# Gate and up units of a two-layer FFN: one 512-column product for the high and low activations, halves summed by VectorE

## The reference

```python
D_MODEL, SEQ, D_FF = 1024, 256, 2816

def swiglu(u, w_gu, w_down):
    gate, up = jnp.split(u @ w_gu, 2, axis=-1)      # w_gu: 1024 x 5632
    return (jax.nn.silu(gate) * up) @ w_down        # w_down: 2816 x 1024

for i in range(DEPTH):                              # DEPTH = 2
    ...                                             # mixer and memory attention
    u = rmsnorm(x, ffn_pre_g[i])
    x = x + rmsnorm(swiglu(u, ffn_w_gu[i], ffn_w_down[i]), ffn_post_g[i])
```

## Time and profile before

| | |
|---|---|
| median of 3 runs | 969.23 us (968.77 to 969.78) |
| the profiled execution | 969.12 us, its span 967.3 us |
| PE busy | 929.6 us, 96% of the span |
| PEld busy | 860.7 us, 89% |
| DVE busy | 562.4 us, 58% |
| ACT busy | 487.9 us, 50% |
| HBM read | 162 MB, 169 GB/s over the span |
| mean granted TensorE clock | 0.986 of full |
| gate and up units of layer 0 | about 353 to 480 us of the span |
| gate and up units of layer 1 | about 770 to 899 us |

### The profile page before, as it was taken

How to read it: one execution, slowest core, us unless ns; L and a number is a source line. 1 busy time by engine, 2 the same in 40 slices (tenths; PEclk the granted TensorE clock), 3 DMA queues, 4 the chain that set the end, 5 groups by cost and what they waited for, 6 DMA issues and landing times.

```text
span 967.3 us, 15639 instructions
## 1 busy us (share of the span) xinstructions
PE 929.6 (96%) x6624; PEld 860.7 (89%) x6624; DVE 562.4 (58%) x645; ACT 487.9 (50%) x670; POOL 36.8 (4%) x51
## 2 busy tenths in 40 slices
PE   8999999989999989999999999999999699999996
PEld 7999987868899889999988899987998599999885
DVE  6788465874565575555544754675754645554443
ACT  6565567854545564344433554666645534434332
POOL 1000001220000000000000220000000000000000
PEclk9999999999999999999999999999999699999999
DMA  8866452234653465555555697434643345555651
GB/s 262 270 191 190 131 162 82 91 126 134 208 186 126 130 210 183 173 175 188 191 184 194 211 272 216 132 130 131 219 143 115 114 141 192 188 174 174 194 197 44
DMA packets 121061, 163.80 MB, mean 169 GB/s; under 512 B 4076, under 2 KB 106916, under 8 KB 121012
## 3 DMA queue, kind: packets, MB, share of 16 engines
q1 hardware_dynamic: 117684, 151.99, 48.4%
q0 software_dynamic: 3328, 11.10, 3.9%
HBM read 162.01 MB, written 1.07 MB: 169 GB/s over the span
## 4 chain that ended last, share of the span: by engine, by line
PE 84%; DVE 9%; ACT 4%; issue 2%; DMA 1%; SPq 0%; POOL 0%; DVEq 0%; ACTq 0%
PE bank L443 76%; DVE w_lo L1142 2%; DVE ntmp L1205 1%; PE bank L740 1%; PE bank L711 1%; DVE x L1208 1%; DVE ntmp L1184 1%; ACT ntmp L851 1%; PE bank L637 1%; PE bank L543 1%; DMA d_pair<-in_ssm_d_dram 1%; DVE stats L1173 1%; DVE stats L1175 1%; PE bank L795 1%; PE bank L785 0%
## 5 line engine op out<-in xcount | busy, mean ns | idle before, releaser
L1142 DVE TENSOR_TENSOR w_lo<-w_raw,w_hi 128x2048 fp32r<-128x2048 f32 x135 | 308.5, 2290 | 225.1 <-ACT w_hi L829 225.0
L443 PE MATMUL bank<-actT_hi,w_hi 128*128 128x256 f32 x1280 | 365.1, 285 | 3.3 <-DVE actT_lo L1192 1.6
L443 PE MATMUL bank<-actT_lo,w_hi 128*128 128x256 f32 x1280 | 363.4, 284 | 0.0
L443 PE MATMUL bank<-actT_hi,w_lo 128*128 128x256 f32 x1280 | 363.4, 284 | 0.0
L829 ACT ACTIVATE w_hi<-w_raw 128x2048 fp32r<-128x2048 f32 x135 | 256.7, 1907 | 105.8 <-DMA w_raw<-in_ffn_w_down_dram 52.6
L443 PEld LDWEIGHTS bank<-actT_hi,w_hi 128*128 128x128 f32 x1280 | 247.0, 193 | 5.3 <-issue 4.6
L443 PEld LDWEIGHTS bank<-actT_lo,w_hi 128*128 128x128 f32 x1280 | 247.0, 193 | 0.1
L443 PEld LDWEIGHTS bank<-actT_hi,w_lo 128*128 128x128 f32 x1280 | 246.9, 193 | 0.0
L443 PE MATMUL bank<-w_lo,hT_hi 128*128 128x512 f32 x176 | 68.5, 389 | 0.0
L443 PE MATMUL bank<-w_hi,hT_hi 128*128 128x512 f32 x176 | 68.5, 389 | 0.0
L443 PE MATMUL bank<-w_hi,hT_lo 128*128 128x512 f32 x176 | 68.5, 389 | 0.0
(11 more groups left out here) (209 smaller groups left out, 1279.6 us busy)
## 6 DMA issues: line engine op xcount, KB each, us to landing
w_raw<-in_ffn_w_gu_dram SPq DMA_DIRECT2D x44, 1024.0 KB, 5.1
w_raw<-in_ffn_w_down_dram SPq DMA_DIRECT2D x22, 1024.0 KB, 4.9
w_raw<-in_ssm_w_in_dram SPq DMA_DIRECT2D x20, 1024.0 KB, 5.3
w_raw<-in_mem_w_kv_dram SPq DMA_DIRECT2D x16, 1024.0 KB, 5.5
w_raw<-in_ssm_w_out_dram SPq DMA_DIRECT2D x8, 1024.0 KB, 4.9
w_raw<-in_mem_w_q_dram SPq DMA_DIRECT2D x8, 1024.0 KB, 5.2
w_raw<-in_mem_w_o_dram SPq DMA_DIRECT2D x8, 1024.0 KB, 4.9
w_raw<-in_w_kv_dram SPq DMA_DIRECT2D x8, 1024.0 KB, 5.9
```

What stands on the lines that cost most here:

```text
L443: ins = pe.matmul(dst, a, b, start=first and n == 0, stop=last and n == len(passes) - 1, skip_group_check=True)
L1142: dve.tensor_tensor(lo[:, s, :], raw[:, s, :], hi[:, s, :].bitcast(F32), ALU.subtract).then_inc(w_lo_done, 1)
```

## The change

The activations now stand as one tensor `actT` with high and low side by side for each k-tile (512 columns). `pair_unit` replaces `t_unit` in the gate and up units: for each column block and k-tile one matmul of 512 columns (high weights against high and low activations) and one of 256 columns (low weights against the high activations) that adds to the second half. Each column block takes a PSUM bank of its own, so a unit fills banks 0 and 1 or 2 and 3 in turn. The product is the sum of the two halves of a bank; VectorE makes that sum with one `tensor_reduce` for each unit, into `gate` or `hval`. Silu then works on `gate` in SBUF, and the product of the two on `hval` in SBUF. Every `t_out` of these units comes from VectorE.

```diff
@@ freed_by
     if name in ("gu0", "gu1"):
-        return "dve" if i % 2 else "act"
+        return "dve"
@@ placement
-        actT_hi = place("actT_hi", [P, KD, S], F32R)
-        actT_lo = place("actT_lo", [P, KD, S], F32R)
+        actT = place("actT", [P, KD, 2, S], F32R)
+        actT_hi, actT_lo = actT[:, :, 0, :], actT[:, :, 1, :]
@@ TensorE
+            def pair_unit(slot, b):
+
+                for c in range(2):
+                    for k in range(KD):
+                        cols = slice(k * TC + c * P, k * TC + (c + 1) * P)
+                        wh, wl = hi[:, slot, cols], lo[:, slot, cols]
+                        pe.matmul(bank[:, b + c, :], wh, actT[:, k].rearrange("p e n -> p (e n)"), start=k == 0, stop=False,
+                                  skip_group_check=True)
+                        ins = pe.matmul(bank[:, b + c, S:2 * S], wl, actT_hi[:, k, :], start=False, stop=k == KD - 1,
+                                        skip_group_check=True)
+                return ins
...
                     for j in range(5):
                         if j:
-                            e, n = free_of_slot(j, i)
-                            pe.wait_ge(t_out[e], n)
+                            pe.wait_ge(t_out["dve"], i * 4 + (d0 + j - 1))
                         if j < 4:
                             pe.wait_ge(w_lo_done, i * 4 + (u0 + j + 1))
-                            t_unit((u0 + j) % SLOTS, (v0 + j) % 2, actT_hi, actT_lo).then_inc(w_used, 1)
+                            pair_unit((u0 + j) % SLOTS, j % 2 * 2).then_inc(w_used, 1)
@@ ScalarE, feed_forward
                 def unit(j, i, per, tile):
 
                     hi_unit(u0 + 2 + j, i, per)
-                    act.wait_ge(w_used, i * 4 + (u0 + j + 1) if per else u0 + j + 1)
                     if j % 2 == 0:
-                        act.activation(gate[:, j // 2 % 2], tiles((v0 + j) % 2), ACT.Silu).then_inc(t_out["act"], 1)
+                        act.wait_ge(t_out["dve"], i * 4 + (d0 + j + 1) if per else d0 + j + 1)
+                        act.activation(gate[:, j // 2 % 2], gate[:, j // 2 % 2], ACT.Silu).then_inc(gate_ready, 1)
                     else:
-                        act.wait_ge(t_out["dve"], i * 2 + (d0 + j // 2 + 1) if per else d0 + j // 2 + 1)
+                        act.wait_ge(h_ready, i * 2 + (g0 + j // 2 + 1) if per else g0 + j // 2 + 1)
                         act.activation(hT_hi[:, tile, :], hval[:, j // 2 % 2], ACT.Copy).then_inc(h_hi, 1)
@@ VectorE, feed_forward
                 def unit(j, i, per, tile):
                     lo_unit(u0 + 2 + j, i, per)
+                    b = j // 2 % 2
+                    halves = bank[:, j % 2 * 2:j % 2 * 2 + 2, :].rearrange("p c (e n) -> p c n e", e=2)
+                    dst = hval if j % 2 else gate
+                    dve.wait_ge(w_used, i * 4 + (u0 + j + 1) if per else u0 + j + 1)
+                    dve.tensor_reduce(dst[:, b], halves, AX.X, ALU.add).then_inc(t_out["dve"], 1)
                     if j % 2:
-                        b = j // 2 % 2
-                        dve.wait_ge(w_used, i * 4 + (u0 + j + 1) if per else u0 + j + 1)
-                        dve.wait_ge(t_out["act"], i * 2 + (a0 + j // 2 + 1) if per else a0 + j // 2 + 1)
-                        dve.tensor_tensor(hval[:, b], tiles((v0 + j) % 2), gate[:, b], ALU.mult).then_inc(t_out["dve"], 1)
+                        dve.wait_ge(t_out["dve"], i * 4 + (d0 + j + 1) if per else d0 + j + 1)
+                        dve.wait_ge(gate_ready, i * 2 + (h0 + j // 2 + 1) if per else h0 + j // 2 + 1)
+                        dve.tensor_tensor(hval[:, b], hval[:, b], gate[:, b], ALU.mult).then_inc(h_ready, 1)
                         dve.wait_ge(h_hi, i * 2 + (h0 + j // 2 + 1) if per else h0 + j // 2 + 1)
                         dve.tensor_tensor(hT_lo[:, tile, :], hval[:, b], hT_hi[:, tile, :].bitcast(F32), ALU.subtract).then_inc(h_lo, 1)
```

More of the change, by code:

```diff
@@ L307, in program @@
         h_hi, h_lo = sem("h_hi"), sem("h_lo")
+        gate_ready, h_ready = sem("gate_ready"), sem("h_ready")
         stored = sem("stored")
@@ L474, in banked @@
                 pe.wait_ge(w_lo_done, u + 1)
+                if name in ("gu0", "gu1"):
+                    pair_unit(u % SLOTS, i % 2 * 2).then_inc(w_used, 1)
+                    return
                 f = t_unit if KIND[name] == "T" else v_unit
@@ L492, in fill_half, with loop_t @@
                     ins.then_inc(w_used, 1)
-            def loop_t(name, iters, free_of_slot):
+            def loop_t(name, iters):
                 u0, v0 = U[(name, 0)], V_OF[(name, 0)]
+                d0 = FREED[v0][1] - 1
                 for e, n in FREED[v0 - 2:v0]:
@@ L749, in feed_forward @@
                 name = f"gu{layer}"
-                a0, d0 = FREED[V_OF[(name, 0)]][1] - 1, FREED[V_OF[(name, 1)]][1] - 1
-                loop_t(name, 5, lambda j, i: (("act", "dve")[j % 2], i * 2 + ((a0, d0)[j % 2] + j // 2)))
+                loop_t(name, 5)
                 for i in (20, 21):
@@ L1054, in feed_forward @@
                 u0, v0 = U[(name, 0)], V_OF[(name, 0)]
-                a0, d0 = FREED[v0][1] - 1, FREED[v0 + 1][1] - 1
+                d0, g0 = FREED[v0][1] - 1, (FT // 2) * layer
                 act.preload_act_table_set("silu_and_others")
@@ L1395, in feed_forward @@
                 name = f"gu{layer}"
-                u0, v0 = U[(name, 0)], V_OF[(name, 0)]
-                a0 = FREED[v0][1] - 1
+                u0 = U[(name, 0)]
+                d0 = FREED[V_OF[(name, 0)]][1] - 1
                 h0 = (FT // 2) * layer
```

## The result

The changed kernel takes 989.5 us (median of 4 runs, 988.78 to 990.5) against 969.5 us before. The ratio is 1.0203, its 95% interval 1.0191 to 1.0216: 2% slower, inside the predicted range and 2.3 us above the predicted 987.2. The profiled execution took 990.1 us with a span of 988.3.

What follows compares the result with a forecast made beforehand. TensorE bounds the kernel before; after the change a ring of waits between VectorE and ScalarE, 12.79 us for two units against TensorE's 11.09, binds. Each layer loses 7.14 + 0.59 + 1.32 = 9.05 us; 969.12 plus 18.1 gives 987.2 us, range 981 to 1000.

Steps and rivals of the forecast that it cites:

- The pace of TensorE before and its possible gain: Gate and up units: 5.546 us a unit in place of 5.755, 9.2 us over 44 units if other engines keep up.
- ring hidden: Rival: VectorE reduces u+1 before the low piece of u+3, so TensorE's 9.2 us gain stays: 960.0 us; 3%.
- The reduce: VectorE's new reduce of 1024 PSUM elements in each gate and up unit: 1.22 us, bounds 0.69 and 2.29.
- that rival: Rival: the strided PSUM read costs two steps an element, so a reduce takes 2.29 us and the kernel 1034 us; 9%.
- The ring: Gate and up units: reduce, Silu or product, high piece, low piece, next reduce wait in turn; 12.79 us for two units.
- Start of a layer: First reduce starts at 358.91 in layer 0, when TensorE is done with the first unit; the ring binds from there.
- The end of a layer: Down0 starts 7.14 us later, then its second and third low pieces come 0.59 and 1.32 us late.
- TensorE's idle time: Sign: TensorE idles 11.7 us in the units and 1.9 in the down part of each layer, some 27 us in both.
- The clock: Granted clock stays 1.00 in the units; rival: short TensorE idle times drop it to 1.2 GHz, 1093 us in all; 2%.
- The layers' sum: Both layers' feed-forward parts together lose 2 x 9.05 = 18.1 us.

Runs made afterwards that it cites:

- e5_lead_three: Changed kernel with ScalarE's high pieces one unit earlier and the wide matmul split in two of 256 columns: 969.7 us.
- e8_low_first: Kernel of e1_lead with the two matmuls of a pair swapped, the 256-column one first: 964.5 us.
- e3_layout: Kernel before with only the placement of the change, actT_hi and actT_lo as halves of one tensor: 969.7 us.
- e6_before_lead: Kernel before with only ScalarE's high pieces one unit ahead in the feed-forward loops: 969.3 us.
- e1_lead: Changed kernel with ScalarE making its high pieces one unit earlier in the feed-forward loops: 962.7 us.
- e7_lead_again: The kernel of e1_lead run once more, nothing changed: 966.2 us.
- e10_lead_third: The kernel of e1_lead run again, on the same chip as the kernel with grouped matmuls: 963.9 us.
- e2_half: Changed kernel with a reduce that reads only the first half of each bank, 512 elements in place of 1024: 965.9 us.

## Why the prediction was right

**The pace of TensorE before and its possible gain.** Right in size for the faster pace: 4.7 and 4.4 us in the two layers against a predicted 4.6 (e5_lead_three against e8_low_first). But the sum took 0.2267 + 0.1199 us for each pair as given, from runs of one length, and the alternating pair goes in many layers at 0.3533. The rival "ring hidden" had 960.0 us for that reason; with an open ring medians of 962.7 to 966.2 came. In the forecast itself it cost nothing, since the ring left room for either pace (11.1 or 11.3 us in 12.8).

**The reduce.** 1.217 us against 1.22, from a row of 512 and the difference of two others. The strided reading of PSUM, the one thing without a row, added nothing, so the 2.29 us and the 1034 us of that rival fall. The Trainium skill ("SBUF — State Buffer", "Door 1: The DMA port swizzle") speaks of slower matmuls with patterns in PSUM that are not contiguous; for VectorE's read of such a pattern this trace shows no price (1.217 us for 1024 elements, where the elementwise operation over 1024 in a row took 1.225).

**The ring.** Right: 12.78 us against 12.79. Its two halves were off by 0.1 us in opposite ways: Silu started 0.03 us behind the end of the reduce (376.45 against 375.20 + 1.22), where I had put 0.14, and the product 0.12 us behind its reduce (382.46 against 381.12 + 1.22), where I had put 0.04. The other steps were as put.

**Start of a layer.** Here a term was missed. I had the first reduce start when TensorE was done with unit 0. In layer 0 the low piece ahead of it in VectorE's list is late, since ScalarE loads a table ahead of its high piece. The rows were there before (the low piece lasts until 359.81, while unit 0 ended at 359), but I didn't hold them against the reduce. First the kernel before, then the change:

```profile
354.28 1.28 ACT L1056 ACT_TABLE_LOAD   x1
357.52 2.29 DVE L1142 TENSOR_TENSOR w_lo<-w_raw,w_hi 128x2048 fp32r<-128x2048 f32 x1 [0.93 <-ACT w_hi L829]
...
360.20 2.29 DVE L1157 TENSOR_TENSOR w_lo<-w_raw,w_hi 128x2048 fp32r<-128x2048 f32 x1 [0.94 <-ACT w_hi L844]
362.41 1.22 DVE L1421 TENSOR_REDUCE gate<-bank 128x512 f32<-128x1024 f32 x1
```

With the 2.68 us of delay of that execution the prediction's 358.91 is 361.59; it started at 362.41, 0.82 us later, at the end of the low piece. A ring that binds from the first turn carries this to the end: 9.05 + 0.82 = 9.87 against 9.8 measured in layer 0. In layer 1 the table is loaded long before unit 0 ends (781.51, against a first reduce at 790.40), and there the loss was 8.4. That is less than 9.05 because the kernel before had a long start at half clock there. The prediction took that start as costing both kernels alike; it did not. The granted clock rose 11.0 us behind the last norm's start in the kernel before (norm at 765.01), 9.5 us in the change and 8.6 in e3_layout and e6_before_lead (norm at 765.36). First before, then e6_before_lead (columns as above):

```profile
774.00:776.00 2.00, 2.00 (x11) 2.00 (x11) 0.51 (x1) 0.00 (x0) 0.00 (x0) 0.51 0.00 0
774.00:776.00 2.00, 2.00 (x19) 2.00 (x18) 2.00 (x2) 0.33 (x1) 0.00 (x0) 1.00 0.00 0
```

The kernel before's 2.4 us more at half clock go with 1.0 us more in the layer (191.3 against 190.2), so the change's 1.5 us less are worth some 0.65 us (an estimate from these distances). With it layer 1 loses 9.05 us at equal clock, as predicted.

**The end of a layer.** The first reduce of the last pair (unit 20) came 490.26 - 362.41 = 127.85 us after the first, against 127.9. TensorE started down0 at 490.49 and its second unit at 496.41, 0.48 us later than 5.44 us a unit would give (predicted 0.59); the third low piece started at 500.64, 4.45 us behind the reduce of unit 21 (predicted 4.56).

**TensorE's idle time.** As a sign the prediction had 27 us of it, 11.7 in the units and 1.9 in the down part of each layer. The rows give less, 16.1 us for the gate units' reduces and 2.3 in the down parts of both layers, because a row of TensorE outlasts its distance to the next one (0.40 against 0.23 us) and covers the start of each wait. By starts, down0 came (490.49 - 361.22) - 21 x 5.546 = 12.8 us later than unit 1 and the faster pace would give, up to 2.2 of it the slower pace (21 x 0.105); in the down part it is 0.48 + 1.22 = 1.7 us. The sign holds in size, but it can't be read from the wait table alone.

**The clock.** Right: 1.00 through the ring's stretch, with TensorE idle for 8.2 of 106 us. The low clock at the start of layer 1's units was there in the kernel before as well: in the earlier trace rows it is at 0.50 in 759 to 764, where TensorE was busy for 1.97 of 5.00 us, and still in 770 to 776, where it was busy all the time. The Trainium skill ("TensorE: Matmul & The Clock Gate", "A second HAM failure mode: psum-queue depth-cycling") warns that short idle times of TensorE between groups of matmuls make the clock swing; that did not come about in this trace's units.

**The 2.3 us between 987.2 and 989.5.** The layers' sum, 18.1 against 18.2, was met in part by luck: the missed 0.8 us of layer 0 was offset by the clock's 0.65 us in layer 1, and neither was in the prediction. The rest of the 21.0 us between the two profiled executions (969.12 and 990.1) is the 2.7 us ahead of layer 0, which the sum could not have, since it started from one execution with a high clock there.

## What to carry to other kernels

When work moves from one engine to another, write down for each engine's list what stands behind each new wait and follow it until it closes on itself; the sum of such a ring, start to start, is a bound of its own, which the busy shares (62% and 49% here) don't show. While such a ring binds, an operation on it costs its full duration each turn, and letting the other engine prepare one unit further ahead can take it off the path; here that cost nothing. Then only is the faster product worth measuring.

## What the runs showed of the hardware that was not expected

- TensorE's pace for a matmul of 512 columns followed by one of 256, each with its own weights, was 0.3467 us or 0.3533 us a pair, steady through a whole layer where nothing interrupted it, at the same granted clock of 1.00. Runs of one length give 0.2267 + 0.1199 = 0.3466. Layer 1 of one kernel had the faster pace in e1_lead and the slower in e7_lead_again and e10_lead_third; layer 0 had the slower one in all three, and the faster one with the narrow matmul first (e8_low_first). The pace also changed within a layer, behind an interruption (e2_half, the change). What chooses is open. It is 2.3 us a layer here.
- Eight wide and then eight narrow matmuls had one pace in both layers of the one profile, in between: 5.59 us a unit.
- A VectorE reduce over two values 256 elements apart in PSUM pays nothing for the jumps: 1.217 us for 1024 elements read and 512 written, where an elementwise operation over 1024 in a row took 1.225, and a reduce of 512 in a row 0.684 (e2_half) whether it wrote 512 values or, at 0.689, two.
- With the instructions of a stretch the same, the granted clock differed between executions of one kernel: 1.00 in 140 to 150 us in e1_lead, 0.83 in e7_lead_again and e10_lead_third. In all twelve traces the part ahead of layer 0's units was the longer the lower the clock was there, by up to 4 us.
